# Forming the low parts of thirteen weight halves a layer by accumulating transfers instead of by VectorE

## The chip, the cores and the metric

The kernel runs on one core of a Trainium2 chip. The metric is the device time of one execution in microseconds; smaller is better. Before the change the median of three runs is 1240.32 us (1240.03 to 1242.2).

## The reference, cut to what matters

The input is 256 tokens of width 1024 in float32. A first block (windowed attention with two kinds of heads and a gated merge) is followed by two layers of a second kind. The change touches only the weights of those two layers:

```python
for l in range(DEPTH_2):                      # 2 layers
    h = _rmsnorm(x, norm_mix[l])
    z = h @ w_in[l]                           # one wide product, split into 15 parts
    (q_n, kc, vc, ks, vs, kw, vw, g_n, q_r, k_r, v_r, g_r, c_a, c_b, m_g) = _split_cols(z)
    o_nsa  = _nsa(...)                        # compressed, selected and windowed attention
    o_ret  = _retention(q_r, k_r, v_r, g_r, ret_gn[l])
    o_conv = _conv_module(c_a, c_b, ...)      # gate, 31 taps of a depthwise convolution, layer norm
    merged = sum over the three branches of sigmoid(m_g) * (branch @ w_branch[l])
    x = x + merged @ w_out[l]
    h2 = _rmsnorm(x, norm_mlp[l])
    x = x + square(relu(h2 @ w_ff1[l])) @ w_ff2[l]
```

All products are of float32 matrices and must come out at about float32 accuracy.

## The kernel before

**Two parts of each number.** TensorE multiplies a rounded type (fp32r). So each operand is split into a high part, the value rounded to that type, and a low part, the rest: low = value - high. A product is the sum of three: high x high, high x low and low x high (lines 883 to 885 for panels made by rows of tokens, 904 to 906 for panels made by columns).

**Halves.** The weights come as panels of 512 output columns. A panel is mostly two halves, `name/0` and `name/1`, of 1 MB each (128 partitions x 2048 numbers). Exceptions: the two halves of `vsg` are 128 x 1120, a branch panel `br..` is one half, a `down` panel eight. In the order of use a layer has these panels: gr, cb, ca, k4, q, vsg; then the eight wide panels qkr, vr, mg0 to mg5 (with w1k and w1v, the weights of the compression, inside qkr and vr); then six branch panels, wo0, wo1, ff0 to ff7, down0, down1. That is 72 halves.

**The path of a half.** SyncE loads half n into one of six slots of `ring` (`load_half`), once the half that lay in the slot six halves before has been used. ACT writes its high part to one of three further places, behind the slots (`round_half`, line 551), once half n-3 has been used by TensorE. VectorE (DVE) subtracts, and the low part takes the place of the loaded half in its slot (`low_half`, line 576). TensorE waits for the count of low parts, `low_ready`, and multiplies. `ring` and `ring_lo` (in the profile `ring_parts`) are the same memory seen as two types. An `act.wait_ge(half_loaded[slot], ...)` and the count `high_ready` join the steps.

**What sets the order.** Each engine has its own list of instructions, written out by hand. `round_after(act, part, half)` puts the rounding of the half three later behind a use, and `lows_to(part, half)` does the same in VectorE's list. In the wide panels, a table (`LAYER_PLAN`) hangs a step of the attention, the retention or the convolution on each of a panel's eight steps k: S is a pair of score products, then logits on VectorE (L2080 to L2084), exp on ACT (L1546, L1547), T transposes (TensorE L933, then ACT L1561), V the product with the values. VectorE does four of the convolution's multiplications for one tap (L2013) at each T and V. It forms one low part at step 2 and one at step 6 of a panel (`lows_at`).

**GpSimd (POOL)** has only the inverse roots of the norms: for a layer, one at its start, one that the retention waits for after panel mg1 (`ret_stats`, then `ret_rstd`), one for the convolution's norm (`conv_stats`), and one for the second norm.

Of the kernel before, what the change touches and what calls it, by code (L numbers as in the profile page):

```python
# [43 lines left out]
SLOTS = 6  # L44
# [53 lines left out]
FIRST_HALVES = halves_of(FIRST_PANELS, ())  # L98
LAYER_HALVES = halves_of(LAYER_PANELS, ("Oc", "Or"))
N_HALVES = len(LAYER_HALVES)  # L100
BY_COLUMNS = ("cb", "ca", "k4", "q", *[f"ff{i}" for i in range(FF_PANELS)])


# [146 lines left out]
HIGH_1 = Turns([h for h, _ in FIRST_HALVES], HI_SLOTS)  # L250
HIGH_2 = Turns([h for h, _ in LAYER_HALVES], HI_SLOTS, HIGH_1.after)
assert N_HALVES % HI_SLOTS == 0
assert sum(PANELS_2.each) % 2 == 0 and sum(HALVES_2.each) % SLOTS == 0


# [54 lines left out]
def block_kernel(nc, a, out):  # L310

    ctx = ExitStack()
    with ctx:
# [3 lines left out]
        def sem(name):  # L317
            return ctx.enter_context(nc.semaphore(name))
# [104 lines left out]
        half_used = sem("half_used")  # L423
        high_ready = sem("high_part_ready")
        low_ready = sem("low_part_ready")
        merged_high = sem("merged_high_part_ready")
        decay_loaded = sem("decay_loaded")
        tile_done = [sem(f"tile{i}_done") for i in range(TILES)]
# [60 lines left out]
        def layer(l):  # L489
            return Part(TILES_2, PANELS_2, HALVES_2, HIGH_2, LAYER_HALVES, l)  # L490

        def count(part, first_block, each, n):

            return n if part.l is None else part.l * each + (first_block + n)
# [22 lines left out]
        def width_of(name):  # L517

            return 4 * 280 if name.startswith("vsg") else 4 * 256 if name.startswith("kava") else HALF

        def places(part, n):


            if n < len(part.halves):
                name = part.halves[n][0]
                slot, before = part.turn("half", name)
                return name, slot, before, part.turns["high"].at[name][0]
            name = LAYER_HALVES[n - len(part.halves)][0]
            slot, before = HALVES_2.at[name]
            if part.l is not None:  # L530
                before = part.l * HALVES_2.each[slot] + (HALVES_2.each[slot] + before)
            return name, slot, before, HIGH_2.at[name][0]
# [5 lines left out]
        def round_half(act, part, n):  # L538

            if past_end(part, n):  # L540
                return
            name, slot, before, hi = places(part, n)
            if n >= HI_SLOTS:
                wait_used(act, part, part.halves[n - HI_SLOTS][0])
            act.wait_ge(half_loaded[slot], before * 16 + 16)
            w = width_of(name)
            if part.l is None and n == 0:
                act.activation(ring_lo[:, SLOTS + hi, 0:w // 2], ring[:, slot, 0:w // 2], ACT.Copy).then_inc(first_high, 1)
                act.activation(ring_lo[:, SLOTS + hi, w // 2:w], ring[:, slot, w // 2:w], ACT.Copy).then_inc(high_ready, 1)
                return  # L550
            act.activation(ring_lo[:, SLOTS + hi, 0:w], ring[:, slot, 0:w], ACT.Copy).then_inc(high_ready, 1)  # L551

        def index_of(part, half):
            return [h for h, _ in part.halves].index(half)
# [6 lines left out]
        def low_half(g, part, n):  # L561

            if past_end(part, n):
                return
            name, slot, _, hi = places(part, n)
            w = width_of(name)
            if part.l is None and n == 0:
                g.wait_ge(first_high, 1)
                g.tensor_tensor(ring_lo[:, slot, 0:w // 2], ring[:, slot, 0:w // 2], ring_lo[:, SLOTS + hi, 0:w // 2], ALU.subtract)\
                 .then_inc(first_low, 1)  # L570
                g.wait_ge(high_ready, 1)
                g.tensor_tensor(ring_lo[:, slot, w // 2:w], ring[:, slot, w // 2:w], ring_lo[:, SLOTS + hi, w // 2:w], ALU.subtract)\
                 .then_inc(low_ready, 1)
                return
            g.wait_ge(high_ready, count(part, len(FIRST_HALVES), N_HALVES, n + 1))
            g.tensor_tensor(ring_lo[:, slot, 0:w], ring[:, slot, 0:w], ring_lo[:, SLOTS + hi, 0:w], ALU.subtract).then_inc(low_ready, 1)  # L576
# [249 lines left out]
        def _(pe):  # L826
# [27 lines left out]
            def wait_parts(part, name):  # L854

                if name == "qa/0":
                    pe.wait_ge(first_low, 1)
                else:
                    pe.wait_ge(low_ready, count(part, len(FIRST_HALVES), N_HALVES, index_of(part, name) + 1))
                return ring_lo[:, SLOTS + part.turn("high", name)[0], :], ring_lo[:, part.turn("half", name)[0], :]  # L860

            def both_parts(part, name):
# [1475 lines left out]
        @block.gpsimd  # L2338
        def _(g):
            def inverse_root(to, of, scale, out_sem, shape_power):  # L2340

                g.sem_inc(taken, 1)
                g.tensor_scalar(to, of, scale, EPS, ALU.mult, ALU.add)
                g.drain()
                g.tensor_tensor(to, to, shape_power, ALU.pow).then_inc(out_sem, 1)

            g.wait_ge(pad_ready, PADS)
            g.wait_ge(squares, 2)
            inverse_root(rstd, ss, 1.0 / D, rstd_root, half_power[:, 0:2])
            g.wait_ge(rstd_root, 1)  # L2350
            g.tensor_scalar(rstd_half, rstd, 0.5, None, ALU.mult).then_inc(rstd_ready, 1)
            for n, p in enumerate(NORMED):
                nh = 2 if p == "kava" else 8
                g.wait_ge(head_sum, NB * (n + 1))
                if n >= 1:
                    g.wait_ge(head_normed, NB * n)
                inverse_root(hr[:, :, 0:nh], hs[:, :, 0:nh], 1.0 / HD, head_rstd,
                             half_power[:, 0:nh].unsqueeze(1).broadcast_to([P, 2, nh]))
            for l in range(LAYERS):
                g.wait_ge(squares, l * 4 + 4)  # L2360
                inverse_root(rstd, ss, 1.0 / D, rstd_root, half_power[:, 0:2])
                g.wait_ge(rstd_root, l + 2)
                g.tensor_scalar(rstd_half, rstd, 0.5, None, ALU.mult).then_inc(rstd_ready, 1)
                g.wait_ge(ret_stats, l + 1)
                inverse_root(brs[:, :, :], bna[:, :, 1:2].rearrange("p (b h) o -> p b (h o)", b=2), 1.0, ret_rstd,
                             half_power[:, 0:4].unsqueeze(1).broadcast_to([P, 2, 4]))
                g.wait_ge(conv_stats, l + 1)
                inverse_root(crs, cna[:, :, 1], 1.0, conv_rstd, half_power[:, 0:2])
                g.wait_ge(squares, l * 4 + 6)
                inverse_root(rstd, ss, 1.0 / D, rstd_ready, half_power[:, 0:2])  # L2370
            g.wait_ge(squares, 4 * LAYERS + 4)
            inverse_root(rstd, ss, 1.0 / D, rstd_ready, half_power[:, 0:2])
# [158 lines left out]
```

## Time and profile before

| | us |
|---|---|
| median of three runs | 1240.32 |
| the profiled execution's own time | 1237.37 |
| its span (first to last instruction) | 1235.5 |
| TensorE busy in the span | 1183.5 |
| VectorE busy | 852.2 |
| ACT busy | 549.5 |
| POOL busy | 35.3 |

The span is what all shares refer to. TensorE's granted clock is 0.99 of full over the whole run. In the rows further down, PE is TensorE's products, PEld its weight loads, DVE VectorE, SP SyncE, and a trailing q means an engine's instruction queue. "idle before" is the time in which an engine had nothing running ahead of an instruction, and the arrow names what ended it.

### The profile page before, as it was taken

What the parts mean: (1) busy time and instruction counts of PE and PEld (TensorE: products, weight loads), DVE (VectorE), ACT (ScalarE), POOL (GpSimd) and SP (SyncE); (2) the same over time, 40 slices, a digit from 0 to 9 for tenths busy, and PEclk for the clock granted to TensorE, in tenths of its full rate; (3) what the DMA queues carried; (4) which work ended last, traced back from release to release, by engine and by line L of the source; (5) the groups of instructions that cost most, each with busy time, mean ns of one, the idle gap of its engine ahead of it and who ended that gap; (6) DMA issues with size and microseconds to landing.
All of it is one profiled execution on the core that took longest, in us unless ns stands there. A gap on an engine that the chain in (4) does not pass through costs nothing.

```text
span 1235.5 us, 17215 instructions
## 1 busy us (share of the span) xinstructions
PE 1183.5 (96%) x6888; PEld 1012.3 (82%) x6888; DVE 852.2 (69%) x1325; ACT 549.5 (44%) x689; POOL 35.3 (3%) x43
## 2 busy tenths in 40 slices
PE   7999999999999798999999999998798999999996
PEld 5788788887997676887999888996676888999885
DVE  4466466556688898787677554698888787776442
ACT  5554565444425444443534433434453543443331
POOL 1122000000000000000000000000000000000000
PEclk9999999999999999999999999999899999999998
DMA  8456545347545233344455555454332444455640
GB/s 303 159 187 230 212 153 168 102 148 256 179 143 205 102 111 129 136 171 170 171 183 194 199 199 197 163 181 159 119 107 103 170 172 171 171 187 189 211 147 34
DMA packets 39467, 206.54 MB, mean 167 GB/s; under 512 B 4003, under 2 KB 13731, under 8 KB 16307
## 3 DMA queue, kind: packets, MB, share of 16 engines
q1 hardware_dynamic: 39052, 205.22, 47.9%
q8 instruction: 55, 0.90, 0.3%
q10 hardware_dynamic: 336, 0.22, 0.1%
q14 instruction: 24, 0.20, 0.0%
HBM read 204.23 MB, written 1.20 MB: 166 GB/s over the span
## 4 chain that ended last, share of the span: by engine, by line
PE 74%; DVE 16%; DVEq 4%; issue 2%; ACT 2%; DMA 0%; POOL 0%; POOLq 0%; ACTq 0%
PE panel L883 16%; PE panel L885 16%; PE panel L884 16%; PE panel L906 6%; PE panel L905 6%; PE panel L904 6%; DVE area L2013 5%; DVE ring_parts L576 4%; PE tile L933 3%; DVEq L2014 2%; PE heads_out L1092 1%; DVEq L2083 1%; ACT ring_parts L551 1%; DVE area L2081 1%; PE tile L991 1%
## 5 line engine op out<-in xcount | busy, mean ns | idle before, releaser
L576 DVE TENSOR_TENSOR ring_parts<-ring,ring_parts 128x2048 fp32r<-128x2048 f32 (+1 forms) x185 | 415.4, 2257 | 156.6 <-ACT ring_parts L551 152.5
L551 ACT ACTIVATE ring_parts<-ring 128x2048 fp32r<-128x2048 f32 (+1 forms) x185 | 348.6, 1888 | 257.7 <-PE panel L885 201.6
L883 PE MATMUL panel<-ring_parts,hT_high 128*128 128x512 f32 (+2 forms) x688 | 282.2, 410 | 15.9 <-DVE ring_parts L576 12.7
L885 PE MATMUL panel<-ring_parts,hT_low 128*128 128x512 f32 (+2 forms) x688 | 267.1, 388 | 0.0
L884 PE MATMUL panel<-ring_parts,hT_high 128*128 128x512 f32 (+2 forms) x688 | 266.1, 387 | 0.0
L904 PE MATMUL panel<-hT_high,ring_parts 128*128 128x256 f32 x704 | 199.4, 283 | 0.0
L906 PE MATMUL panel<-hT_high,ring_parts 128*128 128x256 f32 x704 | 199.2, 283 | 0.0
L905 PE MATMUL panel<-hT_low,ring_parts 128*128 128x256 f32 x704 | 199.2, 283 | 0.0
L883 PEld LDWEIGHTS panel<-ring_parts,hT_high 128*128 128x128 f32 x688 | 130.7, 190 | 56.6 <-issue 30.4
L885 PEld LDWEIGHTS panel<-ring_parts,hT_low 128*128 128x128 f32 x688 | 130.6, 190 | 27.3
L883 PE MATMUL panel<-ring_parts,area_parts 128*128 128x512 f32 x384 | 150.6, 392 | 0.0
L884 PE MATMUL panel<-ring_parts,area_parts 128*128 128x512 f32 x384 | 149.9, 390 | 0.0
L884 PEld LDWEIGHTS panel<-ring_parts,hT_high 128*128 128x128 f32 x688 | 131.3, 191 | 20.2
L885 PE MATMUL panel<-ring_parts,area_parts 128*128 128x512 f32 x368 | 143.7, 391 | 0.0
L904 PEld LDWEIGHTS panel<-hT_high,ring_parts 128*128 128x128 f32 x704 | 135.2, 192 | 0.0
L905 PEld LDWEIGHTS panel<-hT_low,ring_parts 128*128 128x128 f32 x704 | 135.2, 192 | 0.0
L906 PEld LDWEIGHTS panel<-hT_high,ring_parts 128*128 128x128 f32 x704 | 135.2, 192 | 0.0
L2013 DVE SCALAR_TENSOR_TENSOR area<-area,cw 128x256 f32<-128x256 f32 x240 | 100.2, 479 | 2.0
L884 PEld LDWEIGHTS panel<-ring_parts,area_parts 128*128 128x128 f32 x384 | 72.2, 188 | 15.1
L883 PEld LDWEIGHTS panel<-ring_parts,area_parts 128*128 128x128 f32 x384 | 72.2, 188 | 15.1
L885 PEld LDWEIGHTS panel<-ring_parts,area_parts 128*128 128x128 f32 x368 | 69.1, 188 | 14.8
L1659 ACT ACTIVATE area_parts<-area 128x1024 fp32r<-128x1024 f32 x16 | 16.9, 1059 | 98.7 <-DVE area L2310 98.7
(228 smaller groups left out, 1089.3 us busy)
## 6 DMA issues: line engine op xcount, KB each, us to landing
ring<-in_w_layers_dram SPq DMA_DIRECT2D x140, 1024.0 KB, 4.9
ring<-in_w_first_dram SPq DMA_DIRECT2D x40, 1024.0 KB, 5.0
area<-bias_rows SPq DMA_DIRECT2D x16, 160.0 KB, 3.2
ring<-in_w_layers_dram SPq DMA_DIRECT2D x4, 560.0 KB, 3.9
area<-bias_rows SPq DMA_DIRECT2D x16, 96.0 KB, 3.0
area<-bias_rows SPq DMA_DIRECT2D x1, 1536.0 KB, 9.0
area<-in_gains_dram SPq DMA_DIRECT2D x3, 512.0 KB, 5.8
x<-in_x_dram SPq DMA_DIRECT2D x2, 512.0 KB, 4.4
```

What stands on the lines that cost most here:

```text
L551: act.activation(ring_lo[:, SLOTS + hi, 0:w], ring[:, slot, 0:w], ACT.Copy).then_inc(high_ready, 1)
L576: g.tensor_tensor(ring_lo[:, slot, 0:w], ring[:, slot, 0:w], ring_lo[:, SLOTS + hi, 0:w], ALU.subtract).then_inc(low_ready, 1)
L883: pe.matmul(ps[:, b, 0:width], high, hi[:, k, :], start=first, stop=False)
L884: pe.matmul(ps[:, b, 0:width], high, lo[:, k, :], start=False, stop=False)
L885: mm = pe.matmul(ps[:, b, 0:width], low, hi[:, k, :], start=False, stop=last)
L904: pe.matmul(to, hi[:, k, cols], hT_hi[:, k, :], start=(k == 0), stop=False)
L905: pe.matmul(to, hi[:, k, cols], hT_lo[:, k, :], start=False, stop=False)
L906: mm = pe.matmul(to, lo[:, k, cols], hT_hi[:, k, :], start=False, stop=(k == KC - 1))
L933: mm = pe.transpose(ps[0:rows, i * P:(i + 1) * P], source(i), ident[:, :])
L1659: act.activation(hidden_parts()[0][:, 4 * i:4 * i + 4, :], sq[:, i % 2, :].rearrange("p (k t) -> p k t", k=4), ACT.Copy).then_inc(squares_ ...
L2013: v.scalar_tensor_tensor(acc[:, c, :], src, cw[:, c, j:j + 1], acc[:, c, :], ALU.mult, ALU.add)
L2014: v.drain()
```

## The change

Thirteen of a layer's 72 low parts are no longer formed by VectorE: `BY_TRANSFER` is the second halves of cb, ca, k4, q, vsg and of the eight wide panels qkr to mg5. For such a half ACT, right after the high part, writes the negated high part over the loaded half in its slot. Then POOL issues a DMA that reads the same half again from memory and adds it onto the slot: -high + value = low. TensorE waits for this DMA by a semaphore of the slot. All other halves go as before, with VectorE's count adapted.

```diff
+BY_TRANSFER = [f"{p}/1" for p in ["cb", "ca", "k4", "q", "vsg"] + LAYER_WIDE]
...
             act.activation(ring_lo[:, SLOTS + hi, 0:w], ring[:, slot, 0:w], ACT.Copy).then_inc(high_ready, 1)
+            if by_transfer(part, n):
+                act.activation(ring_lo[:, slot, 0:w], ring[:, slot, 0:w], ACT.Copy, scale=-1.0).then_inc(negated, 1)
...
             name, slot, _, hi = places(part, n)
+            if by_transfer(part, n):
+                return
             w = width_of(name)
...
                 if name == "qa/0":
                     pe.wait_ge(first_low, 1)
+                elif part.l is not None and name in BY_TRANSFER:
+                    slot = part.turn("half", name)[0]
+                    pe.wait_ge(low_added[slot], 16 * (part.l * len(TRANSFERS[slot]) + TRANSFERS[slot].index(name) + 1))
                 else:
-                    pe.wait_ge(low_ready, count(part, len(FIRST_HALVES), N_HALVES, index_of(part, name) + 1))
+                    pe.wait_ge(low_ready, lows_by_vector(part, index_of(part, name)))
...
+            def add_low(l, names):
+
+                for half in names:
+                    slot = HALVES_2.at[half][0]
+                    i = index_of(layer(l), half)
+                    w = width_of(half)
+                    g.wait_ge(negated, l * len(BY_TRANSFER) + BY_TRANSFER.index(half) + 1)
+                    g.dma_start(ring_lo[:, slot, 0:w], a["w_layers"][l * N_HALVES + i][:, 0:w], accum_op=ALU.add).then_inc(low_added[slot], 16)
+
             for l in range(LAYERS):
...
                 g.tensor_scalar(rstd_half, rstd, 0.5, None, ALU.mult).then_inc(rstd_ready, 1)
+                until = BY_TRANSFER.index("mg2/1") + 1
+                add_low(l, BY_TRANSFER[:until])
                 g.wait_ge(ret_stats, l + 1)
...
+                add_low(l, BY_TRANSFER[until:])
                 g.wait_ge(conv_stats, l + 1)
```

ACT's list in the panels ahead of the wide ones, before (from the tanh of gr to the gates of vsg; L551 is the rounding of one half):

```order
L1526 ACTIVATE area<-panel,stat 128x512 x2
L551 ACTIVATE ring_parts<-ring 128x2048 x2
L1529 ACTIVATE area<-area 128x1024
L551 ACTIVATE ring_parts<-ring 128x2048 x4
L551 ACTIVATE ring_parts<-ring 128x1120 x2
L551 ACTIVATE ring_parts<-ring 128x2048 x2
L1535 ACTIVATE area<-panel,stat 128x256
```

The same stretch after the change (L558 is the rounding, L560 the new negated copy, L1553, L1556 and L1562 are L1526, L1529 and L1535 of before):

```order
L1553 ACTIVATE area<-panel,stat 128x512 x2
L558 ACTIVATE ring_parts<-ring 128x2048 x2
L560 ACTIVATE ring_parts<-ring 128x2048
L1556 ACTIVATE area<-area 128x1024
L558 ACTIVATE ring_parts<-ring 128x2048 x2
L560 ACTIVATE ring_parts<-ring 128x2048
L558 ACTIVATE ring_parts<-ring 128x2048 x2
L560 ACTIVATE ring_parts<-ring 128x2048
L558 ACTIVATE ring_parts<-ring 128x1120 x2
L560 ACTIVATE ring_parts<-ring 128x1120
L558 ACTIVATE ring_parts<-ring 128x2048 x2
L560 ACTIVATE ring_parts<-ring 128x2048
```

Behind every second rounding stands one more copy of the same size; nothing else changed places.

POOL's list in the first of the two layers, before (the norm's inverse root, the retention's, the convolution's):

```order
L2345 TENSOR_TENSOR stat<-stat 128x2
L2363 TENSOR_SCALAR stat<-stat 128x2
L2343 TENSOR_SCALAR stat<-bna 128x8
L2345 TENSOR_TENSOR stat<-stat 128x8
L2343 TENSOR_SCALAR stat<-cna 128x2
```

And after the change (L2393 is the accumulating DMA; L2370, L2372, L2399 are L2343, L2345, L2363 of before):

```order
L2372 TENSOR_TENSOR stat<-stat 128x2
L2399 TENSOR_SCALAR stat<-stat 128x2
L2393 DMA ring_parts<-in_w_layers_dram 128x2048 x4
L2393 DMA ring_parts<-in_w_layers_dram 128x1120
L2393 DMA ring_parts<-in_w_layers_dram 128x2048 x5
L2370 TENSOR_SCALAR stat<-bna 128x8
L2372 TENSOR_TENSOR stat<-stat 128x8
L2393 DMA ring_parts<-in_w_layers_dram 128x2048 x3
L2370 TENSOR_SCALAR stat<-cna 128x2
```

Ten of the thirteen DMAs (cb/1 to mg2/1) stand ahead of the retention's root, three (mg3/1 to mg5/1) between it and the convolution's. VectorE's list loses thirteen subtractions a layer and keeps its order otherwise.

## Rows read from the trace of the kernel before

**Rows 1.** The page: busy time of the engines, and SyncE's DMA queue.
```profile
PE 1183.5 (96%) x6888; PEld 1012.3 (82%) x6888; DVE 852.2 (69%) x1325; ACT 549.5 (44%) x689; POOL 35.3 (3%) x43
q1 hardware_dynamic: 39052, 205.22, 47.9%
```

**Rows 2.** Stretches: bounds, length, busy (count) by engine, clock, DMA share, GB/s.
```profile
324.00:371.00 47.00, 47.00 (x394) 47.00 (x393) 37.43 (x54) 16.35 (x12) 0.00 (x0) 1.00 0.46 159
347.00:400.00 53.00, 50.59 (x360) 45.89 (x359) 47.34 (x93) 23.45 (x34) 0.00 (x0) 1.00 0.53 184
400.00:450.00 50.00, 42.55 (x240) 34.30 (x240) 45.34 (x117) 23.02 (x48) 0.00 (x0) 0.97 0.32 112
450.00:505.00 55.00, 50.63 (x272) 40.29 (x271) 47.70 (x126) 23.65 (x46) 1.86 (x2) 0.97 0.33 115
600.00:747.00 147.00, 147.00 (x971) 135.56 (x970) 94.07 (x66) 58.42 (x37) 0.00 (x0) 1.00 0.56 195
804.00:857.00 53.00, 50.94 (x362) 46.14 (x361) 47.45 (x93) 23.55 (x34) 0.00 (x0) 1.00 0.53 183
857.00:907.00 50.00, 42.00 (x237) 33.95 (x236) 44.97 (x117) 22.64 (x47) 0.00 (x0) 0.93 0.31 113
907.00:962.00 55.00, 50.68 (x272) 40.23 (x271) 47.80 (x127) 23.67 (x47) 1.86 (x2) 0.97 0.34 116
```

**Rows 3.** Who waited for whom: TensorE's longest (total, times, longest).
```profile
PE panel L883 <- DVE ring_parts L576: 12.7, 7, 3.4
PE tile L933 <- ACT area L1547: 8.8, 6, 2.0
```

**Rows 4.** Groups by line: count, busy, mean ns, idle before them and releaser.
```profile
L576 DVE TENSOR_TENSOR ring_parts<-ring,ring_parts 128x2048 fp32r<-128x2048 f32 (+1 forms) x185 | 415.4, 2257 | 156.6 <-ACT ring_parts L551 152.5
L551 ACT ACTIVATE ring_parts<-ring 128x2048 fp32r<-128x2048 f32 (+1 forms) x185 | 348.6, 1888 | 257.7 <-PE panel L885 201.6
```

**Rows 5.** VectorE in order of time: start, duration, instruction, idle before.
```profile
398.48 2.29 DVE L576 TENSOR_TENSOR ring_parts<-ring,ring_parts 128x2048 fp32r<-128x2048 f32 x1 [2.30 <-ACT ring_parts L551]
...
420.26 4.49 DVE L576 TENSOR_TENSOR ring_parts<-ring,ring_parts 128x2048 fp32r<-128x2048 f32 x2
...
429.34 0.29 DVE L2080 CUSTOM_DVE_ANT_0 area<-tile,area 128x128 f32<-128x128 f32 x1 [1.25 <-PE tile L1231]
...
470.33 0.36 DVE L2176 TENSOR_SCALAR stat<-stat 128x4 f32<-128x4 f32 x2 [2.26 <-POOL stat L2345]
```

**Rows 6.** ACT in order of time: the roundings of ca/1, vsg/1, qkr/1, vr/1.
```profile
330.16 1.91 ACT L551 ACTIVATE ring_parts<-ring 128x2048 fp32r<-128x2048 f32 x1 [3.13 <-PE panel L906]
...
364.72 1.14 ACT L551 ACTIVATE ring_parts<-ring 128x1120 fp32r<-128x1120 f32 x1 [4.62 <-PE panel L906]
...
373.57 1.92 ACT L551 ACTIVATE ring_parts<-ring 128x2048 fp32r<-128x2048 f32 x1 [1.17 <-PE panel L885]
...
398.76 1.91 ACT L551 ACTIVATE ring_parts<-ring 128x2048 fp32r<-128x2048 f32 x1
```

**Rows 7.** TensorE in order of time: the first product of the same halves.
```profile
341.48 0.28 PE L904 MATMUL panel<-hT_high,ring_parts 128*128 128x256 f32 x1
...
373.37 0.29 PE L883 MATMUL panel<-ring_parts,hT_high 128*128 128x280 f32 x1
...
386.91 0.50 PE L883 MATMUL panel<-ring_parts,hT_high 128*128 128x512 f32 x1
...
409.23 0.50 PE L883 MATMUL panel<-ring_parts,hT_high 128*128 128x512 f32 x1 [1.46 <-DVE ring_parts L576]
```

**Rows 8.** DMA issues: queue, count, KB each, median us from issue to landing.
```profile
ring<-in_w_layers_dram SPq DMA_DIRECT2D x140, 1024.0 KB, 4.9
ring<-in_w_layers_dram SPq DMA_DIRECT2D x4, 560.0 KB, 3.9
```

**Rows 9.** POOL in order of time: the norm's root and the retention's.
```profile
317.18 0.70 POOL L2345 TENSOR_TENSOR stat<-stat 128x2 f32<-128x2 f32 x1
...
468.64 1.66 POOL L2345 TENSOR_TENSOR stat<-stat 128x8 f32<-128x8 f32 x1
```

More of the change, by code:

```diff
@@ L252 @@
 assert N_HALVES % HI_SLOTS == 0
+BY_VECTOR = [h for h, _ in LAYER_HALVES if h not in BY_TRANSFER]
+TRANSFERS = {}
+for _half in BY_TRANSFER:
+    TRANSFERS.setdefault(HALVES_2.at[_half][0], []).append(_half)
 assert sum(PANELS_2.each) % 2 == 0 and sum(HALVES_2.each) % SLOTS == 0
@@ L425, in block_kernel @@
         low_ready = sem("low_part_ready")
+        negated = sem("negated_high_part_ready")
+        low_added = [sem(f"low_part_of_slot{i}_added") for i in range(SLOTS)]
         merged_high = sem("merged_high_part_ready")
@@ L551, in round_half, with by_transfer, lows_by_vector @@
             act.activation(ring_lo[:, SLOTS + hi, 0:w], ring[:, slot, 0:w], ACT.Copy).then_inc(high_ready, 1)
+            if by_transfer(part, n):
+                act.activation(ring_lo[:, slot, 0:w], ring[:, slot, 0:w], ACT.Copy, scale=-1.0).then_inc(negated, 1)
+        def by_transfer(part, n):
+            if part.l is None:
+                return n >= len(part.halves) and LAYER_HALVES[n - len(part.halves)][0] in BY_TRANSFER
+            return LAYER_HALVES[n % N_HALVES][0] in BY_TRANSFER
+        def lows_by_vector(part, n):
+            if part.l is None:
+                return min(n + 1, len(FIRST_HALVES)) + sum(h not in BY_TRANSFER for h, _ in LAYER_HALVES[:max(0, n + 1 - len(FIRST_HALVES))])
+            done = sum(h not in BY_TRANSFER for h, _ in LAYER_HALVES[:n + 1]) + sum(h not in BY_TRANSFER for h, _ in LAYER_HALVES[:max(0, n + 1 - N_HALVES)])
+            return len(FIRST_HALVES) + part.l * len(BY_VECTOR) + done
         def index_of(part, half):
```

## The prediction

> **What bounds the kernel now.** I read the page first: TensorE is busy for 1183.5 of 1235.5 us [rows 1], so no change elsewhere can give more than about 52 us. Then I cut the span into stretches [rows 2]. In 600 to 747 us TensorE is busy all the time, and in 324 to 371, the panels cb to q, too: there VectorE's work is hidden. In the wide panels it is not. In the first layer TensorE is idle for 2.4, 7.5 and 4.4 us (53 - 50.59, 50 - 42.55, 55 - 50.63), together 14.2; in the second layer for 2.1, 8.0 and 4.3, together 14.4. In the same stretches VectorE is busy for 47.3 of 53, 45.3 of 50 and 47.7 of 55 us. The list of waits says who ends TensorE's waits there: VectorE's low parts (12.7 us), and exps on ACT (8.8), which themselves wait for VectorE's logits [rows 3]. In the wide panels the granted clock is 0.97 and 0.93 in three of the long stretches [rows 2]; at half clock, a mean of 0.97 over 50 us is 3 us at the lower level, which costs 1.5 us of full-speed work.
>
> The view in order of time tells how VectorE's lateness arises. It waits for ACT before 398.48, for TensorE before 429.34 and for POOL before 470.33 [rows 5]; between these points it runs without a wait worth naming. What is taken out between two of them moves TensorE; what is taken out ahead of a point is lost in the wait at it.
>
> **What goes.** A subtraction is 2.26 us [rows 4] (2.29 for the full size). Thirteen a layer are 28 us of VectorE. Only those behind 398.48 lie on the path: vr/1 and mg0/1 ahead of 429.34, mg1/1 and mg2/1 ahead of 470.33, mg3/1 and mg4/1 behind it, 6 x 2.29 = 13.7 us. One of the two at 420.26 is followed by a wait of 1.25 us for TensorE [rows 5], so I count 12.5. The other seven (cb/1 to qkr/1, and mg5/1) I take at nothing: TensorE is fully busy beside the early ones [rows 2], and the wait of 2.30 us at 398.48 swallows the rest. If that is wrong, the 2.4 us of idle in 347 to 400 are the most that they can add.
>
> **What is added on ACT.** Thirteen negated copies of 1.89 us [rows 4], in line behind the roundings: 24 us a layer, with ACT busy for less than half of each stretch [rows 2]. Their own time is free, but some exps and evictions behind them come up to 1.9 us later, in the chain on which TensorE waits. I take 2.5 us a layer (a little over one full delay), bounds 0 and 6 x 1.9 = 11. VectorE's relief is then 12.5 - 2.5 = 10 us a layer, 20 in all. Its bounds are 0 and, for both layers, the idle time and the slower clock together, 28.6 + 6 = 35.
>
> **What is added on the way of a half.** This is the disputed term. A half may be rounded when the half three before it is used, and is needed two halves later. For ca/1 the rounding starts at 330.16 and TensorE's first product stands at 341.48 [rows 6, 7]: 11.3 us, two halves of 5.7. Rounding and negating take 3.8, so 7.5 us are left for POOL's issue and the DMA. cb/1, k4/1 and q/1 lie alike. The trace has no DMA from POOL and no accumulating one, so I bound its time. From below: a plain load of the same size lands after 4.9 us [rows 8], and no stall follows. From above: queue 1 moved 205.22 MB in 47.9% of 1235.5 us [rows 1], that is 3.0 us of all 16 engines for 1024 KB. The DMA must also read the slot that it adds onto; at the same rate, one after the other, that is 3.0 more. A load is issued with every half used, every 5.7 us, and where the two share the engines wholly it takes another 3.0; POOL's issue is an unknown, and its nearest rows are 0.70 and 1.66 us [rows 9]. Together 4.9 + 3.0 + 3.0 + 1.7 = 12.6. I take 4.9 + 3.0 + 1.5 + 0.7 = 10.1 us: the second read in full because the slot has to be read before it is written, the load by half because the engines' share in these panels is 0.46 [rows 2]. It makes TensorE wait:
> - cb/1, ca/1, k4/1, q/1: 10.1 - 7.5 = 2.6 each, 10.4.
> - vsg/1: 364.72 to 373.37 is 8.65 us, less 2 x 1.14 leaves 6.4 [rows 6, 7]; its DMA is 3.9 [rows 8] + 1.7 + 1.5 + 0.7 = 7.8, so 1.4.
> - qkr/1: 373.57 to 386.91, less 3.8, leaves 9.5: 0.6.
> - vr/1: 398.76 to 409.23, less 3.8, leaves 6.6: 3.5.
> - mg0/1 to mg5/1: nothing. With attention steps between them a half takes 7 to 8 us and two give room. They lose this cover if the DMA takes 12 us or more.
>
> That is 15.9 us a layer, 31.8 in all; bounds 0 and (at 12.6) about 27 a layer, 54.
>
> Nothing in TensorE's waits is queued behind an idle engine otherwise: everything in its list stands behind the stalled product, so a stall is paid in full where it was busy throughout. In POOL's list the retention's root stands behind the DMA of mg2/1, whose negated copy comes in panel mg1, ahead of the statistics; I take nothing for it, at most one issue of 1.7 us.
>
> A rule bears on the disputed term. By the Trainium skill (Collectives: The Full Stack, "The bandwidth ceiling: the fold count and why AG ≠ RS ≠ AR") an adding transfer runs at half the rate of a copying one, not for the arithmetic but because two sources are read on the same ring. This trace has no adding transfer; it is the case of the full 3.0 us for the second read, and without it the stalls would be cb to q nothing, and vr/1 alone 0.5.
>
> **The sum.** 1237.4 (the profiled execution's own time) - 20 + 31.8 = 1249.2. The median of the runs shown is 2.9 us above the profiled execution, so 1252 us.
>
> **The rivals.**
> - *The transfer is fast enough.* If reading the slot goes on beside reading the memory, the DMA lands after about 7.1 us (4.9 + 1.5 + 0.7), less than the 7.5 of the early panels. Then VectorE's relief stays: 1240.3 - 20 = 1220, down to 1206 at its bound; with stalls of 1 us in the early panels and 2 in vr/1, 1240.3 - 20 + 12 = 1232. For it: the engines are busy for only 0.46 of the time in the early panels and 0.32 in the wide ones [rows 2]. Against it: two loads and one adding transfer of 6.0 us would be 12.0 of engine time in the 11.3 us that two early halves take. The point from which it decides: a landing under 9 us after the negated copy. This is the case on the other side.
> - *The transfers are the new bound.* If adding is slower than two reads, say 13 to 14 us from the copy to the landing, the stalls at 13.5 are 4 x 6.0 for cb to q, 5.0 for vsg/1, 4.0 for qkr/1, 6.9 for vr/1 and about 2 for each of mg0 to mg5: 52 a layer, while VectorE's relief is hidden by them and counts for nothing more. That is 1240.3 + 104 = 1344 at worst; at 12 us they are 4.5 x 4 + 3.3 + 2.5 + 5.4 = 29.2 a layer, and 1240.3 + 58.4 - 20 = 1279. Nothing in the trace excludes it, since no such transfer is in it.
> - *Both balance.* At a landing of 8.7 us the stalls are 4 x 1.2 + 0.4 + 2.1 + 0 = 7.3, near the relief of 10 less what ACT's copies take from it: within 3 us of 1240.
>
> **How the numbers follow.** The forecast (a landing of 9.3 to 11 us) has 0.38, and its own range is 1242 to 1270. The fast transfer has 0.37, the slow one 0.17, the balance 0.08. The range 1212 to 1300 leaves out the best corner of the fast case and most of the slow case above 13 us. A measurement of this kernel tells about 0.2%, 2.5 us, from no change. Faster by more: 0.37 of the fast case and 0.02 of the balance, 0.39. The same: 0.06 of the balance and 0.02 from the forecast's lower edge, 0.08. Slower: the rest of the forecast, 0.36, and the slow case, 0.17, together 0.53.
>
> **What would show it.** In the profile of the changed kernel: a DMA row for POOL with its time to landing (about 9.4 behind my issue of 0.7, or under 7, or over 11); in 324 to 380 us TensorE idle for some 12 us before the products of the second halves, ended by a DMA, in steps of about 2.6; in the wide panels TensorE's idle time for VectorE and ACT down from 14 to about 4 us a layer, and VectorE's busy time in the run down by 26 subtractions, 58 us. I am wrong if TensorE stays fully busy in the panels cb to q, or if its idle time in the wide panels goes up, or if it goes down by less than 5 us a layer although VectorE is free.

## The result and the profile after

The changed kernel takes 1257.98 us (median of 4 runs, 1256.32 to 1259.27), the kernel before 1240.17 (1237.04 to 1242.2): the ratio is 1.0156, with a 95% interval of 1.0137 to 1.0175. It is slower by about 18 us. The prediction was 1252, slower. The profiled run took 1257.82 us, with a span of 1256.0.

The page of the changed kernel: busy time by engine, then the queues of SyncE (q1) and GpSimd (q0).
```profile
PE 1192.2 (95%) x6888; PEld 1021.4 (81%) x6888; DVE 797.3 (63%) x1299; ACT 593.3 (47%) x715; POOL 58.3 (5%) x69
q1 hardware_dynamic: 39052, 205.22, 46.6%
q0 software_dynamic: 3744, 26.31, 11.5%
```
Against [rows 1], VectorE is relieved by 54.9 us (26 subtractions) and ACT has 43.8 us more (26 copies). The new queue moves an eighth of the other's bytes, but takes a quarter of its engine time: by its share, time and bytes 0.115 x 1256 / 26.31 x 1.049 MB = 5.8 us of all 16 engines for 1024 KB, where q1 takes 3.0. The landing times stand in the DMA issues of the same kernel (issues, KB each, median us from issue to landing, over the whole run):
```profile
ring_parts<-in_w_layers_dram POOLq DMA_DIRECT2D x24, 1024.0 KB, 9.1
ring<-in_w_layers_dram SPq DMA_DIRECT2D x140, 1024.0 KB, 4.9
ring<-in_w_layers_dram SPq DMA_DIRECT2D x4, 560.0 KB, 5.8
```
Most of the 140 loads have no adding transfer beside them, so their median says little. These are the ten loads (eight of 1024 KB, two of 560 KB) that are issued during the panels cb to vsg of the first layer, first of the kernel before, then of the changed one:
```profile
DMA to landing us min/median/max: 3.7/4.9/5.0
DMA to landing us min/median/max: 3.8/5.2/10.2
```
So loads do land later beside the adding transfers, one of them after 10.2 us, though TensorE waits for none of them there.

TensorE's longest waits (total, times, longest), to be read against [rows 3]:
```profile
PE panel L910 <- DMA ring_parts<-in_w_layers_dram: 13.5, 4, 5.1
PE panel L931 <- DMA ring_parts<-in_w_layers_dram: 11.4, 5, 4.1
PE tile L960 <- ACT area L1574: 6.0, 6, 1.9
```
```profile
PE panel L910 <- DVE ring_parts L600: 3.1, 2, 1.7
```
The waits for VectorE's low parts fell from 12.7 to 3.1 us and those for the exps from 8.8 to 6.0. New are 24.9 us of waits for a DMA, in nine places. These are the four of the first layer, from TensorE's view in order of time, and after them the chain of waits at the last of the four:
```profile
333.77 0.58 PE L931 MATMUL panel<-hT_high,ring_parts 128*128 128x256 f32 x1 [3.90 <-DMA ring_parts<-in_w_layers_dram]
...
360.29 0.42 PE L931 MATMUL panel<-hT_high,ring_parts 128*128 128x256 f32 x1 [1.99 <-DMA ring_parts<-in_w_layers_dram]
...
396.85 0.50 PE L910 MATMUL panel<-ring_parts,hT_high 128*128 128x512 f32 x1 [2.40 <-DMA ring_parts<-in_w_layers_dram]
...
424.35 0.79 PE L910 MATMUL panel<-ring_parts,hT_high 128*128 128x512 f32 x1 [5.08 <-DMA ring_parts<-in_w_layers_dram]
```
```profile
412.03 1.91 ACT ring_parts L560
413.94 0.28 issue
414.23 10.07 DMA ring_parts<-in_w_layers_dram
424.35 0.79 PE panel L910
```
They are the first products of cb/1, k4/1, qkr/1 and vr/1. ca/1, q/1, vsg/1 and mg0/1 to mg5/1 do not wait in this layer. In the chain the negated copy (L560) is followed after 0.28 us by the DMA, and that by the product.

Stretches of the changed kernel (bounds, length, busy by engine, clock, DMA share, GB/s): the panels cb to vsg, the wide panels, and the twelve us from the longest wait's end on.
```profile
324.00:385.30 61.30, 55.41 (x434) 55.01 (x433) 33.12 (x57) 26.78 (x18) 3.49 (x4) 0.94 0.83 226
385.30:539.60 154.30, 139.08 (x741) 112.62 (x740) 112.65 (x308) 81.66 (x137) 9.77 (x12) 0.94 0.64 181
424.00:436.00 12.00, 11.65 (x45) 9.71 (x45) 9.54 (x26) 4.83 (x5) 0.87 (x1) 0.66 0.21 89
```
The same wide panels of the kernel before:
```profile
376.50:527.30 150.80, 136.42 (x741) 109.60 (x741) 130.18 (x316) 69.00 (x129) 2.75 (x4) 0.98 0.37 129
```
The early panels, where TensorE was fully busy at clock 1.00 [rows 2], now have 5.9 us of idle time (61.3 - 55.41) and a clock of 0.94. In the wide panels TensorE is idle for 15.2 us instead of 14.4. Of these, 2.40 + 5.08 = 7.5 end with a DMA, so what VectorE and ACT cause fell from 14.4 to 7.7. Over the whole run (pages of the two kernels) TensorE is idle for 11.8 us more (63.8 against 52.0) and busy for 8.7 us more (1192.2 against 1183.5) with the same 6888 products: more than 40% of the loss is products at the lower clock.

Laid over the kernel before, by the end of each half, the lateness of the first layer builds up so (ends and lateness read from TensorE's products in order of time):

| half | end before | end after | late by | of it new |
|---|---|---|---|---|
| cb/1 | 335.9 | 341.0 | 5.1 | +5.4 (3.9 waiting, 1.3 slower products) |
| ca/1 | 347.4 | 352.5 | 5.1 | 0 |
| k4/1 | 358.9 | 367.8 | 8.9 | +3.7 (2.0 waiting, 1.6 slower products) |
| vsg/1 | 376.6 | 385.5 | 8.9 | 0 |
| qkr/0 | 386.1 | 393.6 | 7.5 | -1.4 |
| qkr/1 | 394.1 | 405.6 | 11.5 | +4.0 |
| vr/1 | 417.2 | 435.9 | 18.7 | +7.2 |
| mg0/0 | 434.6 | 446.7 | 12.1 | -6.6 |
| mg5/1 | 527.3 | 539.6 | 12.4 | +0.3 |

The second layer adds some 8 us in the same places, and 0.3 us of waiting at q/1. Two things stand out. Only every second of the early halves is late in the first layer. And the largest stall, at vr/1, is nearly all given back within one half: before, TensorE waited in front of mg0/0 for VectorE; now VectorE catches up during the DMA's stall.

### The profile page after: what moved, and what is told of

The parts are those of the page before. It is cut to its first block, busy times and chain, and to the rows that moved or that the text cites. A ratio compares the mean times of both kernels' runs of the same rounds, so it can differ in the third digit from the quotient of the medians.

```text
span 1256.0 us, 17241 instructions
## 1 busy us (share of the span) xinstructions
PE 1192.2 (95%) x6888; PEld 1021.4 (81%) x6888; DVE 797.3 (63%) x1299; ACT 593.3 (47%) x715; POOL 58.3 (5%) x69
## 3 DMA queue, kind: packets, MB, share of 16 engines
q0 software_dynamic: 3744, 26.31, 11.5%
## 4 chain that ended last, share of the span: by engine, by line
PE 77%; DMA 7%; DVE 6%; ACT 5%; issue 3%; DVEq 1%; POOL 0%; POOLq 0%; ACTq 0%
PE panel L910 17%; PE panel L912 16%; PE panel L911 16%; DMA ring_parts<-in_w_layers_dram 6%; PE panel L931 6%; PE panel L933 6%; PE panel L932 6%; PE tile L960 4%; ACT ring_parts L558 2%; ACT ring_parts L560 1%; DVE ring_parts L600 1%; PE heads_out L1119 1%; DVE area L2040 1%; PE tile L1018 1%; PE panel L950 1%
## 5 line engine op out<-in xcount | busy, mean ns | idle before, releaser
L558 ACT ACTIVATE ring_parts<-ring 128x2048 fp32r<-128x2048 f32 (+1 forms) x185 | 348.5, 1888 | 253.6 <-PE panel L912 201.4
L600 DVE TENSOR_TENSOR ring_parts<-ring,ring_parts 128x2048 fp32r<-128x2048 f32 x159 | 358.0, 2264 | 165.2 <-ACT ring_parts L558 162.2
L931 PE MATMUL panel<-hT_high,ring_parts 128*128 128x256 f32 x704 | 201.9, 287 | 11.4 <-DMA ring_parts<-in_w_layers_dram 11.4
L933 PE MATMUL panel<-hT_high,ring_parts 128*128 128x256 f32 x704 | 201.2, 286 | 0.0
L931 PEld LDWEIGHTS panel<-hT_high,ring_parts 128*128 128x128 f32 x704 | 137.2, 195 | 12.4 <-DMA ring_parts<-in_w_layers_dram 12.4
L933 PEld LDWEIGHTS panel<-hT_high,ring_parts 128*128 128x128 f32 x704 | 137.1, 195 | 0.0
```

What stands on the lines that cost most here:

```text
L931: pe.matmul(to, hi[:, k, cols], hT_hi[:, k, :], start=(k == 0), stop=False)
L933: mm = pe.matmul(to, lo[:, k, cols], hT_hi[:, k, :], start=False, stop=(k == KC - 1))
```

## The experiments

Theory: the accumulating transfer lands some 10 us behind the copy because the slot is read as well as the memory; VectorE's relief is real but smaller than forecast; the stalls of neighbouring halves are not independent. The rivals: any transfer on this way would be late; ACT's copies cost the time; VectorE's relief is as large as forecast and each early half stalls by itself. Ten of the twelve runs are edits of the changed kernel; g1_vr4 and g4_mg3 are edits of the kernel before.

**How much relief is there, and what do ACT's copies cost?** Two kernels without any transfer. In the first the thirteen low halves are not formed (TensorE multiplies the high half twice, so the time of its products stays); the second makes the negated copies and multiplies them as if they were the low halves.
```diff
 # e8_no_low
-    if by_transfer(part, n):
-        act.activation(ring_lo[:, slot, 0:w], ring[:, slot, 0:w], ACT.Copy, scale=-1.0).then_inc(negated, 1)
-    add_low(l, BY_TRANSFER[:until])
-    add_low(l, BY_TRANSFER[until:])
...                        # TensorE, for a half in BY_TRANSFER:
-    slot = part.turn("half", name)[0]
-    pe.wait_ge(low_added[slot], ...)
+    pe.wait_ge(high_ready, ...)
+    high = ring_lo[:, SLOTS + part.turn("high", name)[0], :]
+    return high, high
 # e7_no_transfer
-    pe.wait_ge(low_added[slot], ...)
+    pe.wait_ge(negated, part.l * len(BY_TRANSFER) + BY_TRANSFER.index(name) + 1)
-    add_low(l, BY_TRANSFER[:until])
-    add_low(l, BY_TRANSFER[until:])
```


> The thirteen low parts are not formed at all (no negated copy, no transfer; TensorE multiplies the high part a second time in their place, so the result is not the reference's). This is VectorE's relief alone. Theory A, that of the prediction: each subtraction taken out behind 398 us shortens the path, 12.5 us a layer, 1240 - 25 = 1215. Theory B: VectorE's lateness is not what holds TensorE in panels mg1 to mg5 (in the changed kernel its lag behind the old one stays at 12.4 us from mg1 to the end of the layer); only the wait ahead of mg0/0 goes, 3 to 5 us a layer: 1230 to 1234.

> The changed kernel with the negated copies but without the thirteen transfers; TensorE waits for the copy (the low parts are then wrong, they are minus the high part). Theory A: relief less the delay by ACT's copies, 1240 - 20 = 1220. Theory B: as without any low parts, and at most 3 us later for ACT's copies, 1230 to 1237. Against the changed kernel's 1258 the rest is what the transfers cost: 38 us by A, 21 to 28 by B.

Without the low halves: 1223.46 us, ratio 0.9871 (0.984 to 0.9902). With ACT's copies: 1228.34, ratio 0.991 (0.9885 to 0.9935). So the most that VectorE's relief can bring is 15.7 us, and the copies take 4.9 of it. VectorE's waits tell where the rest of the freed time went. First the kernel before, then the one without low halves, both from 398 to 505 us:
```profile
DVE ring_parts L576 <- ACT ring_parts L551: 2.3, 1, 2.3
DVE stat L2176 <- POOL stat L2345: 2.3, 1, 2.3
DVE area L2080 <- PE tile L1231: 1.3, 1, 1.3
```
```profile
DVE ring_parts L598 <- ACT ring_parts L558: 6.7, 2, 4.0
DVE area L2106 <- PE tile L1257: 5.2, 3, 3.4
DVE stat L2202 <- POOL stat L2371: 2.3, 1, 2.3
...
DVE bns L2195 <- PE panel L1234: 0.8, 1, 0.8
```
The freed time turned into waits of VectorE's own: 3.9 us more for TensorE's score tiles, 0.8 for a panel of TensorE, 4.4 more for ACT's roundings. And of TensorE's 12.7 us of waits for low parts, 8.0 stayed, 6.7 of them in front of mg0/0 (3.35 in each layer, as before), for a low half that VectorE still forms:
```profile
419.30 0.63 PE L909 MATMUL panel<-ring_parts,hT_high 128*128 128x512 f32 x1 [3.35 <-DVE ring_parts L598]
```
Laid over the kernel before in the same way as above, this kernel is 1.5 us ahead at the end of qkr/0, 3.2 at the end of vr/1 and 6.8 at the end of mg5/1 of the first layer. Nearly half of the gain is made ahead of mg0/0. Part of it is the clock: of the 13.8 us between the two spans, 9.8 are idle time and 4.0 are TensorE's busy time (1183.5 to 1179.5). The half mg3/1 behind a wait of 1.9 us took 9.1 us before and takes 7.5 here, though the wait is as long.

**Is it the addition, or any transfer?** The DMAs stay, with the same bytes from memory, but overwrite the slot instead of adding to it (so the whole half stands where its low part should).
```diff
 # e6_plain
-    g.dma_start(ring_lo[:, slot, 0:w], a["w_layers"][...][:, 0:w], accum_op=ALU.add).then_inc(low_added[slot], 16)
+    g.dma_start(ring_lo[:, slot, 0:w], a["w_layers"][...][:, 0:w]).then_inc(low_added[slot], 16)
```


> The changed kernel with a plain transfer in place of the accumulating one (the slot then holds the whole weights, so the products are wrong). If the second read makes the accumulating transfer slow: landing after 5 to 6.5 us in place of 9.1, no stall above 1 us, and the time of the kernel without transfers, within 4 us. If the issue by POOL, the software queue or the loads beside it make it slow: landing still 8 to 9 us and a time within 5 us of 1258.

It took 1230.07 us, ratio 0.9926 (0.9899 to 0.9953). Its DMA issues and its queue 0:
```profile
ring_parts<-in_w_layers_dram POOLq DMA_DIRECT2D x24, 1024.0 KB, 5.2
...
q0 software_dynamic: 3744, 26.31, 6.4%
```
A copying transfer of the same size, from the same queue, lands after 5.2 us and takes 0.064 x 1229.5 / 26.31 x 1.049 = 3.1 us of engine time: 3.9 us sooner, and 0.54 of the engine time of the adding one. Its queue has the same 3744 packets as that of the adding transfers, so the transfer is not cut finer. The four kernels make a ladder:

| | us | ratio | step |
|---|---|---|---|
| before | 1239 to 1240 | 1 | |
| no low halves | 1223.46 | 0.9871 | relief -1.29% (16.0 us) |
| and ACT's copies | 1228.34 | 0.991 | +0.39% (4.8) |
| and copying transfers | 1230.07 | 0.9926 | +0.16% (2.0) |
| adding ones: the change | 1257.98 | 1.0156 | +2.30% (28.5) |

The third step is not clear of the noise: the intervals of 0.991 and 0.9926 overlap widely. The second is: its runs do not overlap (1222.68 to 1224.59 us against 1228.16 to 1228.52). The times of the two kernels without transfers lie between what the two theories gave for them, 1215 and 1230 to 1234, 1220 and 1230 to 1237.

**Which halves pay?** The list of halves cut down.
```diff
 # e1_wide: BY_TRANSFER = [f"{p}/1" for p in LAYER_WIDE]
 # e2_mg: BY_TRANSFER = [f"{p}/1" for p in LAYER_WIDE[2:]]
 # e3_early: BY_TRANSFER = [f"{p}/1" for p in ["cb", "ca", "k4", "q", "vsg"]]
 #           until = len(BY_TRANSFER)     # all of a layer's DMAs ahead of the retention's root
```


> Only the eight wide panels' second halves by transfer. In the changed kernel the early panels cost 5.3 us (cb/1) and 3.8 us (k4/1) of the first layer and 5.8 and 1.9 of the second, 16.8 in all. If stalls are independent, this kernel takes 1258 - 17 = 1241. If a stall gives the halves behind it room that qkr/1 and vr/1 lose now, it takes 1243 to 1247.

> Only mg0/1 to mg5/1 by transfer: none of them stalls TensorE in the changed kernel, so nothing is paid for the transfers. Theory A: five of the six subtractions on the path go, less ACT's delays, 8 us a layer: 1224. Theory B: the wait ahead of mg0/0 is shortened only by what VectorE does ahead of it, and vr/1's subtraction is still there: 1236 to 1241, the same as before.

> Only cb/1, ca/1, k4/1, q/1 and vsg/1 by transfer. Nothing is gained there, since TensorE is busy throughout, so the time is 1240 plus the stalls. If each of cb/1 to q/1 stalls by itself by 2.6 us and vsg/1 by 1.4 (the prediction's sum): 1240 + 24 = 1264. If a stall lies inside the next one's way from rounding to use and gives it the same room, only every second one stalls: about 4 us plus 1.5 at the low clock at cb/1 and 2 to 4 at k4/1 a layer, 1240 + 17 = 1257.

The eight wide halves alone: 1237.59 us, ratio 0.9991 (0.9977 to 1.0005), no difference, and below both expectations (1241, 1243 to 1247). mg0/1 to mg5/1 alone: 1237.51, ratio 0.998 (0.9965 to 0.9995), hardly a gain. The five early ones alone: 1258.9, ratio 1.0156 (1.0124 to 1.0188), the whole loss of the change. In the wide panels relief and stall cancel; in the early panels there is nothing to relieve and the stall is paid in full. Of the two theories for mg0/1 to mg5/1 alone, that of the prediction (1224) fell.

**Are the early stalls independent?** If each early half stalls by itself, cb/1 and k4/1 alone cost half of what the four do. If a stall gives the next transfer its room, either pair costs about as much as all.
```diff
 # e4_cb_k4: BY_TRANSFER = [f"{p}/1" for p in ["cb", "k4"]]
 # e5_ca_q:  BY_TRANSFER = [f"{p}/1" for p in ["ca", "q"]]
 # both:     until = len(BY_TRANSFER)
```


> Only cb/1 and k4/1 by transfer. Independent stalls: half of the five's cost. Coupled stalls: the same time as with all five (1257), since ca/1, q/1 and vsg/1 cost nothing once these two stall; TensorE waits about 4 us for cb/1 and 2 to 4 for k4/1.

> Only ca/1 and q/1 by transfer, which cost nothing in the changed kernel. Independent: they again cost nothing, 1240. Coupled: with cb/1 and k4/1 no longer late they stall themselves, 2 to 3.5 us each and 1.5 us of low clock: 1240 + 14 to 20.

cb/1 and k4/1 alone: 1256.0 us, ratio 1.0138 (1.0112 to 1.0164). ca/1 and q/1 alone: 1253.64, ratio 1.0113 (1.0085 to 1.0142). Each pair costs 14 to 17 us by itself, and all five together 19: they are coupled. The trace of the kernel with ca/1 and q/1 shows that these, which do not wait in the changed kernel, wait when nothing ahead of them does:
```profile
344.44 0.39 PE L931 MATMUL panel<-hT_high,ring_parts 128*128 128x256 f32 x1 [1.96 <-DMA ring_parts<-in_w_layers_dram]
...
369.50 0.39 PE L931 MATMUL panel<-hT_high,ring_parts 128*128 128x256 f32 x1 [1.76 <-DMA ring_parts<-in_w_layers_dram]
```
The reason stands in ACT's and GpSimd's views of the changed kernel: the rounding, the copy and the DMA issue of ca/1.
```profile
329.91 1.91 ACT L558 ACTIVATE ring_parts<-ring 128x2048 fp32r<-128x2048 f32 x1 [3.13 <-PE panel L933]
331.73 1.89 ACT L560 ACTIVATE ring_parts<-ring 128x2048 fp32r<-128x2048 f32 x1
```
```profile
333.93 0.89 POOL L2393 DMA_DIRECT2D ring_parts<-in_w_layers_dram  x1 [10.00 <-ACT ring_parts L560]
```
The rounding of ca/1 starts at 329.91, as TensorE begins to stall for cb/1 (329.87 to 333.77). So the stall, and the slower products behind it, lie inside the way of ca/1, whose first product comes at 346.6 instead of 341.48 [rows 7]: it has 13.0 us from the end of its copy instead of 7.5, and needs 0.3 to the issue and 9.0 to the landing.

Waits alone do not make the price. In the kernel with cb/1 and k4/1, TensorE waits 3.73 and 1.99 us in the first layer, 5.7 together, but is 9.4 us later at the end of vsg/1 (0.2 of it from before these panels). The rest is for the most part the clock:
```profile
324.00:381.00 57.00, 51.28 (x400) 50.88 (x399) 34.88 (x54) 18.82 (x13) 1.22 (x2) 0.94 0.59 170
```
Its granted clock over these 57 us was 0.94 instead of 1.00 [rows 2], that is 6.8 us at 1.2 GHz instead of 2.4, worth 3.4 us of work. Each of the two halves behind a wait took 7.5 us instead of 5.9. Whether a given wait brings the dip is not settled: behind the 1.96 us of ca/1 above the half took 6.0 us, behind the 1.76 of q/1 7.5.

**Is it VectorE's order or its load?** The change's trace suggested that the wait in front of mg0/0 hangs on the place of one low half (vr/0 in the table of VectorE's lows), and a wait in mg3 on the place of one rounding on ACT. Both can be moved in the kernel before for nothing, and put together with the six transfers of mg0/1 to mg5/1, the only list with a gain clear of the noise.
```diff
 # g1_vr4, on the kernel before
-    lows_at.update({("vr", 0): "qkr/1", ("vr", 2): "w1k", ("vr", 5): "vr/0", ("vr", 7): "w1v"})
+    lows_at.update({("vr", 0): "qkr/1", ("vr", 2): "w1k", ("vr", 4): "vr/0", ("vr", 7): "w1v"})
 # g4_mg3, on the kernel before
+    elif s == 1 and p == "mg3":
+        round_after(act, part, "mg2/1")
...
-    round_after(act, part, f"{p}/1")
+    if p != "mg2":
+        round_after(act, part, f"{p}/1")
 # on the changed kernel: g3_vr4_mg is e2_mg's list with g1's edit, g5_all the same with g4's edit too
```


> The kernel before, with one low half of the vr panel formed by VectorE one step earlier, in the middle of its eight tap products instead of behind the head sums and the gelu steps. In the trace of before TensorE waited 3.35 us for this half in layer 1 (product at 422.70 us), though ScalarE had rounded it by 413.37. Theory 1 (the wait that the changed kernel gave back at mg0/0 belongs to VectorE's order, not to its load): the wait goes, but VectorE reaches the gelu's L2089 some 2.2 us later, on which the TensorE transposes at 418.83 hang, so the net gain is 3.35 - 2.2 = about 1.1 us a layer, 1 to 3 us in all: 1237 to 1239. Rival (VectorE's load alone counts, its order does not): the wait only moves from the one place to the other and the time is within 1 us of before.

> The kernel before, with ScalarE's rounding behind panel mg2 moved behind the second exponential pair of mg3's first step. In the trace of before this rounding (487.47 to 489.37 us) stands between the two exponential pairs, and TensorE waited 1.89 us for the second (490.30), then ran at the lower clock for 7 products of 0.43 us instead of 0.23. Theory 2 (behind VectorE's relief it is ScalarE's order that holds TensorE): the wait goes in both layers, with the clock dip behind it, so 1.9 to 3.3 us a layer, less what VectorE's taps (until 492.04) hold back of the next step: 3 to 6 us in all, 1234 to 1237. Rival (VectorE holds the next step anyway): the wait turns up at VectorE's score sums behind it, and the time stays within 1 us of before.

> The transfers of mg0 to mg5 alone, with the low half of the vr panel one step earlier as in the run above. If the two act in different places, their gains add: the transfers of mg0 to mg5 alone gave 0.998, the earlier low half should give 1 to 3 us, together 1234 to 1237. If both relieve the same VectorE stretch, no more than the larger of the two: 1237 to 1238.

> The transfers of mg0 to mg5, the low half of the vr panel one step earlier and ScalarE's rounding behind mg2 one step later, together. If the three act in different places: 1230 to 1234, under both kernels. If VectorE's relief had been what the moved rounding needed, more than the sum; if they share one stretch, 1235 to 1237.

None gained: g1_vr4 0.9999 (0.9987 to 1.001), g4_mg3 1.0002 (0.9988 to 1.0016), g3_vr4_mg 1.0037 (1.0022 to 1.0053), g5_all 1.0003 (0.9991 to 1.0015). For g1_vr4 and g4_mg3 the theories of the reordering fell, and both rivals held. For the two sums neither expectation came true: g3_vr4_mg (1243.39) and g5_all (1239.56) lie above all that was forecast for them. In g1_vr4 TensorE's waits read:
```profile
PE tile L933 <- DVE area L2089: 7.9, 2, 4.2
PE panel L883 <- DVE ring_parts L576: 5.9, 5, 1.5
```
The wait for low parts fell from 12.7 to 5.9, and the one for the gelu's L2089, which the low half now delays, rose from 3.4 to 7.9 us. In g4_mg3 the wait of 1.89 us in mg3 did go: mg3/1 ended 2.5 us earlier. But mg4/0 ended at the same time as before, because VectorE's next score sums did not move. The row of before and that of g4_mg3:
```profile
499.27 0.29 DVE L2080 CUSTOM_DVE_ANT_0 area<-tile,area 128x128 f32<-128x128 f32 x1 [0.38 <-issue]
```
```profile
499.29 0.29 DVE L2083 CUSTOM_DVE_ANT_0 area<-tile,area 128x128 f32<-128x128 f32 x1 [0.38 <-issue]
```
So these two moves only choose where TensorE waits. That VectorE's load alone sets the time instead is not shown: the six transfers of mg0/1 to mg5/1 take six subtractions a layer off it and gain 0.2%. Why g3_vr4_mg is even slower than the six transfers alone is open: it has a wait of 4.4 us in two places for ACT's L1603 that neither part has by itself in this size (g5_all has 6.0). Of the kernels that compute the reference none beat the kernel before by more than the 0.2% of the six transfers.

## Why the prediction came out as it did

The sign and the time (1252 for 1258) came out, and the disputed term with them, but partly by errors that cancel.

**The landing: right in sum, by terms that cancel.** Predicted were 10.1 us from the end of the copy. The chain above has 0.28 + 10.07 = 10.4, but that is one of the slower ones: the median is 0.3 + 9.1 = 9.4, just inside the forecast's 9.3 to 11. The copying transfer measures the terms one by one. It lands 5.5 us (0.3 + 5.2) after the copy, where I had 4.9 + 1.5 + 0.7 = 7.1 for all but the addition; the load beside and the issue were priced at 2.2 and cost 0.6. The addition brings 3.9 us, where I had 3.0. That term decided, and that the addition costs it is shown: 5.8 us of engine time against 3.0 for a load and 3.1 for the copying transfer. That the cost is the second read and not the arithmetic was my argument, and no run here separates the two. The rule cited (the Trainium skill, Collectives: The Full Stack, "The bandwidth ceiling: the fold count and why AG ≠ RS ≠ AR", on adding transfers at half the rate because two sources are read) is stated there for collectives; it agrees with the trace, 0.54 to 0.52 of the rate.

**The rival of a fast transfer: out.** It had almost the forecast's chance (0.37). Its range of time, 1220 to 1232, holds what the copying transfer gave (1230.07): the addition alone stands between the two cases. The upper end was meant for stalls that the copying transfer does not have; it lands there because the relief is smaller. What spoke for it, engines busy for less than half the time [rows 2], was no evidence. The engines' share in the early panels went to 0.83 of the time, still short of full, and TensorE stalled all the same.

**The stalls: the sum near, the places wrong.** The step that failed is "cb/1, ca/1, k4/1, q/1: 10.1 - 7.5 = 2.6 each". I compared each transfer with a room read from the kernel before, as if the others did not stall. In fact cb/1 waits 3.90, k4/1 1.99, ca/1 and q/1 nothing (and vsg/1 nothing where I had 1.4): 5.9 for the five, not 11.8. The kernel with ca/1 and q/1 alone shows that the room itself was read rightly: there the way of ca/1 takes 0.3 + 9.36 us, 2.2 more than the 7.5, and TensorE waits 1.96 for it. Of the wide halves, qkr/1 waits 2.40 (I had 0.6) and vr/1 5.08 (3.5); mg0 to mg5 nothing, as predicted. The relief itself took their room: qkr/0 ran 1.4 us faster ahead of qkr/1 (8.3 us instead of 9.7), and the room of vr/1 was read up to a product that had waited 1.46 us for VectorE [rows 7], a wait that the change removes. Together 13.4 in the first layer, 24.9 in both, where I had 31.8. The upper bound was added up wrongly: at a landing of 12.6 us the same rooms give 33 us a layer and 67 in all, not 27 and 54.

**Left out: the clock.** I priced idle time alone. Behind the waits the products ran at the lower clock; that is 1.3 and 1.6 us for cb/1 and k4/1. For the transfers as a whole the pages of two profiled runs tell it: from the kernel with the copies alone to the changed one the span grows by 29.6 us (1226.4 to 1256.0), 18.9 of it idle time (24.9 of waits for the DMA, less other waits that they replace) and 10.7 slower products (1181.5 to 1192.2 busy). That the sum agrees with the 31.8 of the prediction is luck. In the bound for the relief, the lower clock was counted in three stretches where [rows 2] has four (0.97, 0.97, 0.93, 0.97), which makes 8 us, not 6.

**The relief: too large.** Net of ACT's copies I took 10 us a layer, 20 in all; the kernel without transfers gained 1239.13 - 1228.34 = 10.8. The copies were right (2.5 a layer taken, 4.9 in all measured). What failed is "between these points it runs without a wait worth naming. What is taken out between two of them moves TensorE": six subtractions taken out, 13.7 us, opened new waits of VectorE for TensorE and ACT, 9.1 us in the layer, which the trace of before does not show. I had set off only the one that was already there (1.25 us). Nor was the way to qkr/1 worth nothing: 1.5 us of the gain is there at the end of qkr/0. The relief fell short by 9.2 us and the transfers cost 2.2 less; take off the 1.2 us by which the kernel before was faster beside these runs (1239.13 for 1240.3), and that is the 6 us by which the result lies above the prediction.

By place it looks worse than in sum. The prediction makes the wide panels gain 10 - 4.1 us a layer, 12 in all; with the wide transfers alone nothing was gained (1237.59, 0.9991). It makes the early ones cost 23.6; alone they cost 19 (1258.9).

**The signs to look for.** "TensorE idle for some 12 us before the products of the second halves" in the early panels was 5.9; "down from 14 to about 4 us a layer" for VectorE and ACT in the wide panels was 14.4 to 7.7; VectorE's busy time fell by 54.9 us (58 predicted). One sign of being wrong, that TensorE's idle time in the wide panels goes up, did appear in the first layer (14.4 to 15.2): it fits the relief that was too large and the stalls there that were too small.

## What to carry to other kernels

A room read from the trace of before is valid for one late transfer where nothing ahead of it changes, not for a row of them: simulate the row, since the stall of one lies inside the way of the next, and price the waits with the lower clock behind them. Where the change also relieves the engine that held things up, take its waits out of the room first. Relief on an engine that waits for nobody is not worth its busy time: the engines behind it can be close, and leaving the work out altogether (one run) tells the most that it can bring, before anything is built to replace it. Move work onto another way only where the engine that it leaves sets the time; the same transfers that broke even in the wide panels cost 1.5% in panels where VectorE had been hidden.

## What the runs showed of the hardware

- An adding transfer from memory onto a slot takes 5.8 us of all 16 engines for 1024 KB and lands after 9.1 us (median); the copying one from the same queue 3.1 and 5.2. Its issue takes GpSimd 0.87 us, that of the copying one 0.54.
- Loads beside it landed later: in the panels cb to vsg of the first layer after 3.8 to 10.2 us, median 5.2, where the kernel before has 3.7 to 5.0, median 4.9. The 560 KB loads of vsg took 5.8 us instead of 3.9 [rows 8], and 6.0 in the kernel where cb/1 and k4/1 alone were transfers.
- Waits were often followed by TensorE products at the lower clock: 0.66 on average over the twelve us from the end of the wait of 5.08 us on, and a half of 7.2 to 7.5 us instead of 5.9 behind those of 3.9 and 2.0. The length of the wait does not tell it: 1.96 us was followed by a half of 6.0 us, 1.76 by one of 7.5. The clock of the whole profiled run fell from 0.99 to 0.979.
